# Full-array products with a packed moving side in the inner levels of a blocked triangular inverse

## What is computed

```python
def _wkv_step(S, inp):
    r, w, k, v, kk, b = inp
    sa = jnp.einsum('bhvk,bhk->bhv', S, -kk)
    S = S * w[:, :, None, :] + sa[..., :, None] * b[:, :, None, :] + v[..., :, None] * k[:, :, None, :]
    y = jnp.einsum('bhvk,bhk->bhv', S, r)
    return S, y
```

## Time and profile before

| | us |
|---|---|
| median of 3 runs (1875.41 to 1878.2) | 1875.71 |
| the profiled execution | 1879.94 |
| its span, first to last instruction | 1878.2 |
| PE busy | 1542.3 (82%) |
| PE weight load busy | 880.0 (47%) |
| DVE busy | 648.0 (35%) |
| ACT busy | 304.9 (16%) |
| POOL busy | 63.6 (3%) |

### The profile page before, as it was taken

One profiled execution on the slowest core, in us unless ns is written; L12 is line 12 of the kernel. 1 busy time (PEld: TensorE's weight loads), 2 busy tenths in 40 slices (PEclk: granted clock), 3 DMA queues, 4 the chain that ended last, 5 costly groups with the idle time before them and its releaser, 6 DMA issues.

```text
span 1878.2 us, 24556 instructions
## 1 busy us (share of the span) xinstructions
PE 1542.3 (82%) x8870; PEld 880.0 (47%) x8870; DVE 648.0 (35%) x1288; ACT 304.9 (16%) x704; POOL 63.6 (3%) x103
## 2 busy tenths in 40 slices
PE   7999999999999999999996675666757667576574
PEld 4676767676767676767752231222312223122121
DVE  6746565656565656410121120111201112010013
ACT  2323232323232323100112000000000000000012
POOL 1101010101010101000000000000000000000000
PEclk9999999999999999999997887888878888788787
DMA  7323232323232323374589999999999999999995
GB/s 286 109 100 113 92 120 82 120 82 120 82 120 82 120 82 120 110 292 165 204 373 426 429 426 429 429 428 428 429 428 427 429 429 429 427 429 430 428 403 212
DMA packets 71904, 510.35 MB, mean 272 GB/s; under 512 B 20496, under 2 KB 23696, under 8 KB 37808
## 3 DMA queue, kind: packets, MB, share of 16 engines
q1 hardware_dynamic: 71808, 509.60, 67.2%
q0 software_dynamic: 48, 0.12, 0.0%
HBM read 499.87 MB, written 9.82 MB: 271 GB/s over the span
## 4 chain that ended last, share of the span: by engine, by line
PE 41%; DMA 34%; DVE 16%; issue 4%; ACT 2%; SPq 1%; DVEq 1%; ACTq 0%
DMA arena<-w_up 22%; DVE arena L1424 16%; DMA arena<-w_down 12%; PE ps_PJ L723 11%; PE ps_C L1069 8%; PE ps_PJ L923 7%; ACT arena L1152 2%; SPq L560 1%; PE ps_C L1120 1%; PE ps_SB L1120 1%; PE ps_YB L1120 1%; PE ps_RT L1120 1%; PE ps_C L696 0%; PE ps_PJ L1023 0%; PE ps_SB L852 0%
## 5 line engine op out<-in xcount | busy, mean ns | idle before, releaser
L723 PE MATMUL ps_PJ<-arena 128*128 128x320 f32 x1792 | 536.6, 437 | 0.0
L1069 PE MATMUL ps_C<-arena 128*32 128x512 f32 x2048 | 285.1, 719 | 178.4 <-DMA arena<-w_gate 110.3
L723 PEld LDWEIGHTS ps_PJ<-arena 128*128 128x128 f32 x1792 | 324.7, 190 | 124.6 <-issue 17.9
L1424 DVE TENSOR_TENSOR arena<-arena,ps_PJ 128x512 f32<-128x512 f32 (+2 forms) x112 | 73.5, 657 | 614.7 <-PE ps_PJ L1023 495.3
L1069 PEld LDWEIGHTS ps_C<-arena 128*32 128x32 f32 x2048 | 79.3, 130 | 377.4 <-issue 375.0
L1152 ACT ACTIVATE arena<-arena 32x160 f32<-32x160 f32 (+9 forms) x350 | 146.6, 419 | 322.0 <-DVEq L422 134.7
L1424 DVE TENSOR_TENSOR arena<-arena 128x512 f32<-128x512 f32 (+12 forms) x311 | 161.8, 520 | 73.5 <-ACTq L422 41.2
L1152 ACT ACTIVATE arena<-ps_C 128x128 f32<-128x128 f32 (+3 forms) x68 | 27.4, 403 | 893.2 <-PE ps_C L1069 530.7
L923 PE MATMUL ps_PJ<-arena 128*128 128x320 f32 x512 | 142.4, 433 | 1.0 <-DVEq L422 1.0
L923 PEld LDWEIGHTS ps_PJ<-arena 128*128 128x128 f32 x512 | 95.5, 190 | 40.2 <-issue 3.3
L1424 DVE TENSOR_TENSOR arena<-ps_PJ,arena 128x512 f32<-128x512 f32 x32 | 22.1, 692 | 258.0 <-PE ps_PJ L1016 257.9
(11 more groups left out here) (181 smaller groups left out, 1175.7 us busy)
## 6 DMA issues: line engine op xcount, KB each, us to landing
arena<-w_down SPq DMA_DIRECT2D x64, 2048.0 KB, 21.5
arena<-w_gate SPq DMA_DIRECT2D x61, 2048.0 KB, 20.4
arena<-w_up SPq DMA_DIRECT2D x61, 2048.0 KB, 20.1
arena<-win SPq DMA_DIRECT2D x59, 1024.0 KB, 4.8
arena<-w_out SPq DMA_DIRECT2D x16, 1024.0 KB, 7.0
arena<-w_gate SPq DMA_DIRECT2D x6, 1024.0 KB, 8.0
arena<-xT SPq DMA_DIRECT2D x8, 640.0 KB, 7.4
arena<-s_ret SPq DMA_DIRECT2D x8, 512.0 KB, 3.8
```

Source lines behind the costliest of these rows:

```text
L723: last = mm(pj(j)[:, 0:T], wt[j % NSLOT][:, kt, :], hT[:, kt, :], start=kt == 0, stop=kt == KT - 1)
L1069: last = mm((GB, UB)[u][h * CAP:(h + 1) * CAP, :], xg[:, kt, h * CAP:(h + 1) * CAP], w[h](k), start=kt == 0, stop=kt == KT - 1)
L1424: ins = build(*args)
```

## The change

Levels 1 to 4 use another form of product. The unmasked blocks `Ac` are spread once a pair into block-diagonal `Ad`, at the head of step u0. Step i then multiplies, for each chunk, the full 128x128 `Ad` as weights with the packed 128x32 `Uc`; DVE multiplies the result with the level's mask as it leaves PSUM, into the packed `Zp`. Step j multiplies `Ud` (128x128 weights) with `Zp` (128x32 moving). `Ud` now holds the transposed inverse, so DVE transposes `Uc` blockwise (TR, into `Vc`) ahead of each spread. The PE transposes k1 to k4, their ACT copies, and POOL's masking into `Am` are gone. In the plan xv comes after j3, and rqb after i3. In the set-up step mk one blockwise transpose becomes a smaller one and a copy.

```diff
 PLAN:
-    "q": "@v ax am -va u0 | cv us0 | | k1 i1 | zs1 xb | j1 pd | ds1 | k2 i2",
-    "kr": "@q | rqa j2 zs2 xk | | rqb k3 i3 | ds2 xv | j3 | | k4 i4",
+    "q": "@v ax am -va u0 | cv us0 | | i1 | zs1 xb | j1 pd | ds1 | i2",
+    "kr": "@q | rqa j2 zs2 xk | | i3 rqb | ds2 | j3 xv | | i4",
 PE:
                 elif s[0] == "i":
+                    pe.wait_ge(inverse, NINV * p + 2 * int(s[1]))
                     for c in range(NC):
-                        o = b[quarter[c], 0:P] if k < INNER else b[quarter[c], 0:HD]
-                        last = mm(o, Am[:, k - 1, c, :] if k < INNER else A5[:, c, :],
-                                  Ud[:, c, :, :] if k < INNER else Ud[:, c, 0:NB32:2, :], start=True, stop=True)
+                        last = mm(b[:, c * BK:(c + 1) * BK], Ad[:, c, :, :], Uc[:, c, :], start=True, stop=True)
                     last.then_inc(full(s), 1)
                 elif s[0] == "j":
+                    wait_freed(pe, "i" + s[1], p)
+                    pe.wait_ge(inverse, NINV * p + 2 * int(s[1]) + 1)
-                        for q in range(NB32):
-                            last = mm(b[quarter[q], 0:P], V2[:, q, :], Zd[:, q, :, :], start=True, stop=True)
+                    for c in range(NC):
+                        last = mm(b[:, c * BK:(c + 1) * BK], Ud[:, c, :, :], Zp[:, c, :], start=True, stop=True)
 ACT:
-                elif s in ("k1", "k2", "k3", "k4"):
-                    wait_filled(act, s, p)
-                    A(V2[:, :, :], bank(s)[:, 0:P].rearrange("p (b j) -> p b j", b=NB32), ACT.Copy).then_inc(free(s), 1)
 DVE:
                 elif s == "u0":
                     dve.wait_ge(done("ac"), 2 * p + 1)
+                    spread(Ad, Ac).then_inc(inverse, 1)
                     TT(Vc[:, :, :], Ac[:, :, :], inner[0][:, None, :].broadcast_to([P, NC, BK]), ALU.mult)
                     TT(Vc[:, :, :], Vc[:, :, :], unit[:, None, :].broadcast_to([P, NC, BK]), ALU.add)
                     TR(Uc.rearrange("p c j -> p (c j)"), Vc.rearrange("p c j -> p (c j)")).then_inc(inverse, 1)
-                    spread(Ud, Uc).then_inc(inverse, 1)
+                    spread(Ud, Vc).then_inc(inverse, 1)
                 elif s in ("i1", "i2", "i3", "i4"):
                     wait_filled(dve, s, p)
-                    spread(Zd, bank(s)[:, 0:P].rearrange("p (b j) -> p b j", b=NB32)).then_inc(free(s), 1)
+                    TT(Zp[:, :, :], bank(s)[:, 0:P].rearrange("p (c j) -> p c j", c=NC),
+                       inner[int(s[1])][:, None, :].broadcast_to([P, NC, BK]), ALU.mult).then_inc(free(s), 1)
                 elif s in ("j1", "j2", "j3", "j4"):
                     wait_filled(dve, s, p)
                     TT(Uc[:, :, :], Uc[:, :, :], bank(s)[:, 0:P].rearrange("p (c j) -> p c j", c=NC), ALU.add).then_inc(free(s), 1).then_inc(inverse, 1)
-                    spread(Ud, Uc).then_inc(inverse, 1)
+                    if s == "j4":
+                        spread(Ud, Uc).then_inc(inverse, 1)
+                        return
+                    TR(Vc.rearrange("p c j -> p (c j)"), Uc.rearrange("p c j -> p (c j)"))
+                    spread(Ud, Vc).then_inc(inverse, 1)
 POOL, step am:
-                    pool.wait_ge(done("ac"), 2 * p + 1)
-                    for k in range(1, INNER):
-                        TT(Am[:, k - 1, :, :], Ac[:, :, :], inner[k][:, None, :].broadcast_to([P, NC, BK]), ALU.mult).then_inc(lmk, 1)
```

More of the change, by code:

```diff
@@ L39 @@
     "C1": ["g1", "j1", "j2", "j3", "j4", "j5", "a0", "a1", "a2", "a3"],
[1 row of a table removed]
+    "C2": ["g2", "k5", "s0", "s1", "s2", "s3"],
     "SB": ["zw", "za", "ss", "g4", "zs1", "ds1", "zs2", "ds2", "rs0", "rs1", "bs", "gg", "as", "us"],
@@ L187, in cut @@
             return x.rearrange("p (c n) -> p c n", **axes) if axes else x
-        Zd = inv[:, 0:512].rearrange("p (b c j) -> p b c j", b=NB32, c=NC)
+        Ad = inv[:, 0:512].rearrange("p (c b j) -> p c b j", c=NC, b=NB32)
         Z5 = cut(512, 64, c=2)
-        Am = inv[:, 640:1152].rearrange("p (k c j) -> p k c j", k=INNER - 1, c=NC)
         Ac = cut(1152, 128, c=NC)
@@ L198, in build_program @@
         V = cut(2560, NCH * P, c=NCH)
-        V2 = cut(3200, 128, c=NB32)
+        Zp = cut(3200, 128, c=NC)
         V2d = inv[:, 3328:3584].rearrange("p (h c j) -> p h c j", h=2, c=NC)
@@ L356, in build_program @@
         vchain, achain, pchain = sem("vector_chain"), sem("scalar_chain"), sem("pool_chain")
+        NINV = 2 * INNER + 1
         N_TILE = {n: i for i, n in enumerate(TILES)}
@@ L761, in step @@
                     k = int(s[-1])
-                    pe.wait_ge(lmk, (INNER + 1) * p + k)
+                    pe.wait_ge(lmk, 2 * p + k)
                     if k == 1:
@@ L772, in step @@
                     mm(b[:, 0:P], V[:, NC, :], Zs, start=True, stop=True).then_inc(full(s), 1)
-                elif s[0] == "k":
-                    pe.wait_ge(inverse, 2 * (INNER * p + int(s[1])) - 1)
+                elif s == "k5":
+                    pe.wait_ge(inverse, NINV * p + 2 * INNER)
                     nc.tensor.transpose(b[:, 0:P], Uc[:, :, :], ident).then_inc(full(s), 1)
-                elif s[0] == "i":
[L777 to L782, removed]
-                    for c in range(NC):
-                        o = b[quarter[c], 0:P] if k < INNER else b[quarter[c], 0:HD]
-                        last = mm(o, Am[:, k - 1, c, :] if k < INNER else A5[:, c, :],
-                                  Ud[:, c, :, :] if k < INNER else Ud[:, c, 0:NB32:2, :], start=True, stop=True)
+                elif s == "i5":
+                    pe.wait_ge(inverse, NINV * p + 2 * INNER + 1)
+                    pe.wait_ge(done("ac"), 2 * p + 2)
+                    for c in range(NC):
+                        last = mm(b[quarter[c], 0:HD], A5[:, c, :], Ud[:, c, 0:NB32:2, :], start=True, stop=True)
+                    last.then_inc(full(s), 1)
+                elif s[0] == "i":
+                    pe.wait_ge(inverse, NINV * p + 2 * int(s[1]))
+                    for c in range(NC):
+                        last = mm(b[:, c * BK:(c + 1) * BK], Ad[:, c, :, :], Uc[:, c, :], start=True, stop=True)
+                    last.then_inc(full(s), 1)
+                elif s == "j5":
+                    wait_freed(pe, "i5", p)
+                    wait_freed(pe, "k5", p)
+                    for h in range(2):
+                        last = mm(b[quarter[2 * h], 0:P], Z5[:, h, :], V2d[:, h, :, :], start=True, stop=True)
@@ L787, in step @@
                     last.then_inc(full(s), 1)
                 elif s[0] == "j":
[L789 to L792, removed]
-                        for q in range(NB32):
-                            last = mm(b[quarter[q], 0:P], V2[:, q, :], Zd[:, q, :, :], start=True, stop=True)
-                    else:
-                        for h in range(2):
-                            last = mm(b[quarter[2 * h], 0:P], Z5[:, h, :], V2d[:, h, :, :], start=True, stop=True)
+                    wait_freed(pe, "i" + s[1], p)
@@ L1600, in step @@
                         RED(folded[:, k, :], whole(lvl[k]), AX_X, ALU.add)
-                    TR(packed[:, 0:INNER, :].rearrange("p k j -> p (k j)"), folded[:, 0:INNER, :].rearrange("p k j -> p (k j)"))
+                    TR(packed[:, 0, :], folded[:, 0, :])
+                    CP(packed[:, 1:INNER, :], folded[:, 1:INNER, :])
                     RED(unit, whole(ident), AX_X, ALU.add)
```

## The result

The changed kernel takes 1892.31 us (median of 6 runs, 1891.97 to 1894.07) against 1875.68 for the kernel before (6 runs): 16.6 us longer, a ratio of 1.0089 with a 95% interval of 1.0076 to 1.0102. The forecast was 1890.5, in a range of 1880 to 1898.

A forecast was written before the change was run, and what follows sets the result against it. PE's work and waits were taken to bound each pair: 0.76 + 0.93 = +1.69 us, first pair +2.93, together 14.8 us, giving 1890.5 us against the median 1875.71 (1894.7 on the profiled execution); range 1880 to 1898.

The forecast's parts named there:

- What bounds the kernel: In the loop over pairs, PE's work plus its waits sets the length; a pair's gain or loss reaches the end undiminished.
- The first pair: First pair of the loop: the two old waits were absent there, so nothing is got back and it grows +2.93 us.
- from there to rs0 (j1 to j4): Level-by-level sum over steps i and j of a pair, both old waits taken as gone: +0.76 us.
- The price of a step: Each new step i or j on PE: eight loads and MATMULs at 0.105 us, 0.84 us, whatever the columns.
- Rival 2: Steps i and j: weight loads hide, a step costs 0.22 us, 34.7 less, about 1856 us; chance 0.06.
- rival 3: Steps i and j: loads show, 0.165 each, 1.32 us a step, 27 more, about 1917 us; chance 0.03.
- The old steps: PE cost before the change: 0.55 us for j1 with its changes of form, 0.66 for k2 and i2.
- The waits at j3 and i4: PE's waits for VectorE at levels 3 and 4, 0.65 and 0.59 us in all pairs but the first, would go.
- rival 4: At j3 and i4 the waits stay, DVE late by its new transpose: 8.7 more, 1899 us; chance 0.05.
- The start on VectorE: Head of u0: the new spread, 0.69 plus a 0.24 gap, delays us0 and so zs1 by 0.93 us a pair.
- rival 1: Before zs1: VectorE's start is off the path, the 0.93 hidden; +5.7 in all, 1881.4 us; chance 0.14.
- What costs nothing: ACT's dropped copies, POOL's dropped masks and DVE's evened work in a pair cost nothing; 0 to 0.8 us in all.

The follow-up runs named there:

- e4: The changed kernel with the moving side of the level 1 to 4 products widened from 32 to 128 columns, same result: 1894.6 us.
- e8: The kernel before with rs0 one projection part later, so a part stands between j4 and rs0: 1879.6 us against 1877.8, pair 93.18.
- e2: The changed kernel with the old order again, rqb ahead of i3 and xv ahead of j3: 1892.6 us, pair 94.72.
- e6: The changed kernel with zs1 and xb one projection part later, just ahead of j1: 1887.1 us, ratio to before 1.0052, pair 94.00.
- e9: The changed kernel with POOL making the four old masks again, which nothing reads: 1894.8 us against 1892.3, pair 94.92.
- e7: The kernel before with xk behind kr's copy, xv behind j4, and zs1 and xb one part later: 1864.8 us against 1877.8, pair 91.37.
- e3: The changed kernel with the spread into Ad made by POOL in step am, not by VectorE in u0: 1893.7 us.

## Why the prediction was right, step by step

**What bounds the kernel, and that the shift is passed on.** Held: pairs longer by 1.89, the output projection 16.2 later and of the same length, the median 16.6 longer. The first pair, forecast +2.93, ends 3.1 later. That the loads issued by PE's progress carry the shift on was argued and not tested.

**One pair, in three stretches.** A pair is taken from rs0 to rs0; these are the lines that it starts with, before and after, and it ends at 373.80 and 382.27:

```profile
280.96 0.62 PE L831 MATMUL ps_SB<-arena 128*24 128x128 f32 x16
```

```profile
287.55 0.64 PE L831 MATMUL ps_SB<-arena 128*24 128x128 f32 x16
```

| from, to | before | after | change | forecast |
|---|---|---|---|---|
| rs0 to the first step of the inverse | 70.61 | 70.79 | +0.18 | 0 |
| from there to the end of zs1 | 2.34 | 2.99 | +0.65 | +0.93 |
| from there to rs0 (j1 to j4) | 19.89 | 20.94 | +1.05 | +0.76 |

The last two rows missed by -0.28 and +0.29, and what is left of the miss is the first row.

**The price of a step.** Forecast 0.84, from the rows of the same shape. Measured 0.81, with 0.08 behind it: 0.89; j4, with the change of form behind it, 0.91. The term was under-sized by 0.05 for each step but j4. That is the +0.29 of the third row, 2.3 us in all; i1's share does not count, as it goes into the wait at zs1. The prediction read the start of the group that follows and not the length of that group, in which the uncovered load is paid. That columns do not bind is shown by e4. Rival 2, loads that hide, and rival 3, 0.165 for each, are out: 0.10 each.

**The old steps.** The 0.55 and 0.66 were right as costs; e8 shows that about 0.3 us of them is the excursion into narrow weights.

**The waits at j3 and i4.** They went, as forecast, and rival 4 is out. Of the reasons that the prediction gave, the shorter eviction and that i4 needs the sum alone suffice (e2); the order does nothing.

**The start on VectorE.** The mechanism held: rival 1, a hidden start, is out, and e6 shows that PE's wait was real. The size forecast was 0.93, from 0.69 and a gap of 0.24. In the trace the transpose of u0 ends 0.6 later than it did, measured from the last product ahead of u0. The missing 0.33 is for the most part what POOL no longer takes from VectorE there: 0.24, as the two small products take 0.62 alone and took 0.86; e9 gave back 0.22 of it. The other 0.09 is the gap, which comes out at 0.15 when the products' own times are taken from the 1.46. Behind us0 some 0.06 come on top, because zs1 starts 0.21 and not 0.11 after the transpose of us0 (360.83 and 353.47); this makes the 0.65 of the table. "What costs nothing" was thus wrong in one point: POOL's masks were not on the path, but they slowed an engine that was.

**Form and waits apart.** e6 and e7 are the two forms rid of their waits. They differ by 94.00 - 91.37 = 2.63 us a pair and by 784.5 - 763.0 = 21.5 at the output projection: this is what the new form costs, with the two places outside the inverse that are told of below. The wait at zs1 in the changed kernel is worth 790.0 - 784.5 = 5.5, and the waits of the kernel before 773.8 - 763.0 = 10.8. That 21.5 + 5.5 - 10.8 gives the shift of 16.2 is so by construction, as the same four starts are subtracted; what the runs add is the size of each part. So the waits did not decide the sign: even the full 10.8 got back does not pay for the products.

**Why the number came so close.** Partly luck. A step priced too low (+2.3) and a start priced too high (-2.3 or so) cancelled; the 1.4 us between the forecast's 14.8 and the 16.2 is the first row of the table, on which the prediction was silent.

What stays open: this 0.17 to 0.18 us a pair lies for the most part in two places outside the inverse. A product of line 810 takes 0.29 in place of 0.22, and the part ahead of step mu 1.34 in place of 1.26. e6 has both and e7 neither. The cause was not found.

## What to carry to other kernels

Here a float32 product with 128-column weights cost 0.22 us with its surroundings, whether 32 or 128 columns moved. It was cheaper to put the narrow operand on the weight side and run four beside each other on quarters of the array: 0.36 against 0.81 for the same four products, and 0.55 against 0.89 with what they cost around them. Where a rewrite of the products seems to remove waits, first try to remove them by the order of the steps alone; here that was worth 11 us at the output projection without touching a product (10.8; 13 in the medians), but only in an order made for the form at hand, in which no engine's bulk work (here ACT's moves) stands ahead of a copy that PE needs. When pricing a step from a timeline, read the length of the group behind it too.

## What the runs showed of the hardware

- Eight MATMULs with 128-column weights took 1.97 us with the part behind them, with 32 moving columns and with 128 (e4). With 32 the first weight load of that part began 0.02 us before its products, with 128 it began 0.11 before.
- VectorE is slowed while POOL runs float32 products between SBUF operands beside its own: VectorE's spread of 128x512 took 0.99 in place of 0.69 us (e3), its three products in u0 1.68 in place of 1.46 (e9), and two 1.39 beside one large one on POOL (e3), 0.86 beside small ones, 0.62 alone.
- An excursion from 128-column weights to narrow ones and back cost 0.35 us with nothing else changed (e8).
